# Stick-breaking attention scores: four f32 products per head against eight fp32r products

## What is computed

```python
def stick_breaking_attention(q, k, v):
    """A[t,s] = sigmoid(z_ts) * prod_{s<j<t} (1 - sigmoid(z_tj)), s < t."""
    z = jnp.einsum('bhqd,bhkd->bhqk', q_blk, kf) * scale
    mask = key_pos < qpos
    log1m = jnp.where(mask, jax.nn.log_sigmoid(-z), 0.0)
    excl = lax.cumsum(log1m, axis=3, reverse=True) - log1m
    a = jnp.where(mask, jnp.exp(jax.nn.log_sigmoid(z) + excl), 0.0)
    return jnp.einsum('bhqk,bhkd->bhqd', a, vf)
```

## Time and profile before

| | us |
|---|---|
| median of 3 runs | 2076.29 |
| lowest, highest | 2075.66, 2077.76 |
| the profiled execution's own time | 2076.51 |
| its span in the profile | 2074.7 |
| TensorE busy | 2026.1 |
| DVE busy | 919.0 |
| ACT busy | 909.0 |
| POOL busy | 848.9 |

### The profile page before, as it was taken

How to read it: one execution, slowest core, us unless ns; L and a number is a source line. 1 busy time by engine, 2 the same in 40 slices (tenths; PEclk the granted TensorE clock), 3 DMA queues, 4 the chain that set the end, 5 groups by cost and what they waited for, 6 DMA issues and landing times.

```text
span 2074.7 us, 23325 instructions
## 1 busy us (share of the span) xinstructions
PE 2026.1 (98%) x9356; PEld 1653.8 (80%) x9356; DVE 919.0 (44%) x1436; ACT 909.0 (44%) x1254; POOL 848.9 (41%) x672
## 2 busy tenths in 40 slices
PE   7999999989999998899999999999999999999999
PEld 6778778868888886788887888888877778888887
DVE  5633224244301315788785454155064544531551
ACT  6455444343223323664655443244266644432441
POOL 1243344436544543333333454444441244444442
PEclk9999999999999999999999999999999999999999
DMA  6122222323333332121212233333311222332332
GB/s 249 48 87 65 78 77 76 92 71 112 92 102 93 100 99 64 51 72 52 71 62 71 85 108 101 93 94 100 94 42 30 80 71 92 101 102 82 112 92 71
DMA packets 51659, 178.09 MB, mean 86 GB/s; under 512 B 5728, under 2 KB 8928, under 8 KB 51424
## 3 DMA queue, kind: packets, MB, share of 16 engines
q1 hardware_dynamic: 51552, 176.61, 27.3%
HBM read 174.49 MB, written 2.10 MB: 85 GB/s over the span
## 4 chain that ended last, share of the span: by engine, by line
PE 93%; DVE 3%; ACT 2%; POOL 1%; issue 1%; DMA 0%; SPq 0%; ACTq 0%
PE ps_gemm L225 24%; PE ps_gemm L227 23%; PE ps_gemm L226 23%; PE ps_attend L225 3%; PE ps_attend L227 3%; PE ps_attend L226 3%; PE ps_attend L1428 2%; PE ps_attend L756 1%; PE ps_attend L2208 1%; PE ps_attend L741 1%; PE ps_attend L2274 1%; PE ps_attend L2209 1%; PE ps_attend L258 1%; PE ps_gemm L1414 0%; PE ps_attend L1457 0%
## 5 line engine op out<-in xcount | busy, mean ns | idle before, releaser
L2467 POOL TENSOR_TENSOR weights_low<-weights_raw,weights_high 128x512 fp32r<-128x512 f32 (+1 forms) x334 | 423.1, 1267 | 1204.4 <-ACT weights_high L200 1203.9
L225 PE MATMUL ps_gemm<-normed_high,weights_high 128*128 128x512 f32 x1672 | 666.4, 399 | 14.2 <-DVE normed_low L287 12.0
L227 PE MATMUL ps_gemm<-normed_low,weights_high 128*128 128x512 f32 x1672 | 652.7, 390 | 0.0
L226 PE MATMUL ps_gemm<-normed_high,weights_low 128*128 128x512 f32 x1672 | 652.4, 390 | 0.0
L200 ACT ACTIVATE weights_high<-weights_raw 128x1024 fp32r<-128x1024 f32 (+1 forms) x341 | 340.8, 1006 | 462.1 <-PE ps_attend L227 220.0
L2468 POOL TENSOR_TENSOR weights_low<-weights_raw,weights_high 128x512 fp32r<-128x512 f32 (+1 forms) x334 | 441.3, 1321 | 0.0
L225 PEld LDWEIGHTS ps_gemm<-normed_high,weights_high 128*128 128x128 f32 x1672 | 315.3, 189 | 85.9 <-DVE normed_low L287 14.4
L226 PEld LDWEIGHTS ps_gemm<-normed_high,weights_low 128*128 128x128 f32 x1672 | 315.4, 189 | 66.4 <-issue 3.8
L227 PEld LDWEIGHTS ps_gemm<-normed_low,weights_high 128*128 128x128 f32 x1672 | 314.7, 188 | 66.3
L225 PE MATMUL ps_gemm<-operands_high_low,weights_high 128*128 128x512 f32 x552 | 217.5, 394 | 2.8 <-POOL weights_low L2468 2.4
L227 PE MATMUL ps_gemm<-operands_high_low,weights_high 128*128 128x512 f32 x552 | 215.7, 391 | 0.0
(11 more groups left out here) (283 smaller groups left out, 2086.0 us busy)
## 6 DMA issues: line engine op xcount, KB each, us to landing
weights_raw<-weights_full SPq DMA_DIRECT2D x317, 512.0 KB, 3.6
weights_raw<-weights_short SPq DMA_DIRECT2D x24, 128.0 KB, 2.0
residual<-x_tiles SPq DMA_DIRECT2D x4, 512.0 KB, 6.9
out_tiles<-residual SPq DMA_DIRECT2D x8, 256.0 KB, 2.1
parameters<-params SPq DMA_DIRECT2D x1, 1559.5 KB, 11.2
scratch<-memory_tiles SPq DMA_DIRECT2D x2, 512.0 KB, 5.7
scratch<-positions SPq DMA_DIRECT2D x1, 256.0 KB, 11.4
parameters<-params SPq DMA_DIRECT2D x1, 136.5 KB, 2.2
```

Of the source, the lines that this page charges most:

```text
L225: t.op.matmul(out, m.wh[:, c:c + P], xh, start=start and n == 0, stop=False, skip_group_check=True)
L226: t.op.matmul(out, m.wl[:, c:c + P], xh, start=False, stop=False, skip_group_check=True)
L227: ins = t.op.matmul(out, m.wh[:, c:c + P], xl, start=False, stop=stop and n == len(pairs) - 1, skip_group_check=True)
L2467: g.op.tensor_tensor(m.wl[:, a], m.raw[:, a], m.wh[:, a].bitcast(F32), ALU.subtract)
```

## The change

Each f32 product of the scores becomes two fp32r products. The first is stacked: 128 rows of contraction, in which the keys' tile holds the head's high keys in its own 64 partitions and its low keys in the other 64, and the queries' tile holds the high queries twice. It yields high times high plus low keys times high queries. The second has 64 rows: high keys times low queries. Low times low is left out.

For this ACT makes, per pair, four 64x512 copies of q (high queries of both heads, own rows and then the other rows) and two of k; DVE makes two low parts of q (into a new tile `ql`) and two low parts of k. Two stack tiles per head lie in unused tiles of `operands_high_low`. TensorE waits for both (`q_both` of ACT, `k_low` of DVE) before the scores of a head. On ACT one more weight unit is copied (`first + 4` in place of `first + 3`) before `act_stick_out`.

```diff
+        self.ql = sb("queries_low", TILE, F32R)
...
+def stick_stacks(m, hh):
+
+
+    return (m.high_tile(6), m.high_tile(7))[hh], (m.high_tile(19), m.high_tile(23))[hh]
+
+
+def own_and_other(hh):
+    return slice(64 * hh, 64 * hh + 64), slice(64 - 64 * hh, 128 - 64 * hh)
+
+
+def act_stick_queries(m, s, i):
+    q = stick_tiles(m)[0]
+    s.wait_ge(*m.V.at("stick", "q", i))
+    for own in (True, False):
+        for hh in range(2):
+            rows = own_and_other(hh)
+            ins = s.op.activation(stick_stacks(m, hh)[1][rows[0 if own else 1], :], q[rows[0], :], ACT.Copy)
+        ins.then_inc(*m.A.mark("stick", "q_high" if own else "q_both", i))
+
+
+def act_stick_keys(m, s, i):
+    k = stick_tiles(m)[1]
+    s.wait_ge(*m.V.at("stick", "k", i))
+    for hh in range(2):
+        own, _ = own_and_other(hh)
+        ins = s.op.activation(stick_stacks(m, hh)[0][own, :], k[own, :], ACT.Copy)
+    ins.then_inc(*m.A.mark("stick", "k_high", i))
+
+
+def dve_stick_parts(m, v, i, what):
+
+    src = stick_tiles(m)[0 if what == "q" else 1]
+    v.wait_ge(*m.A.at("stick", what + "_high", i))
+    for hh in range(2):
+        own, other = own_and_other(hh)
+        keys, queries = stick_stacks(m, hh)
+        out, high = (m.ql[own, :], queries[own, :]) if what == "q" else (keys[other, :], keys[own, :])
+        ins = v.op.tensor_tensor(out, src[own, :], high.bitcast(F32), ALU.subtract)
+    ins.then_inc(*m.V.mark("stick", what + "_low", i))
...
 def pe_stick_scores(m, t, i, hh):
...
-    t.wait_ge(*m.V.at("stick", "k", i))
+    t.wait_ge(*m.A.at("stick", "q_both", i))
+    t.wait_ge(*m.V.at("stick", "k_low", i))
     for kb in (0, 1, 3, 2):
-        w = S - kb * P
-        t.op.matmul(zb[:, ZOFF[kb]:ZOFF[kb] + w], k[r:r + 64, kb * P:(kb + 1) * P], q[r:r + 64, kb * P:S],
-                    start=kb != 3, stop=False, skip_group_check=True)
+        out, sl = zb[:, ZOFF[kb]:ZOFF[kb] + S - kb * P], slice(kb * P, (kb + 1) * P)
+        t.op.matmul(out, keys[:, sl], queries[:, kb * P:S], start=kb != 3, stop=False, skip_group_check=True)
+        t.op.matmul(out, keys[own, sl], m.ql[own, kb * P:S], start=False, stop=False, skip_group_check=True)
...
-    high_to(m, s, first + 3)
+    high_to(m, s, first + 4)
     if i:
         act_stick_out(m, s, i - 1)
+    act_stick_queries(m, s, i)
     high_to(m, s, first + 5)
+    act_stick_keys(m, s, i)
     act_stick_softplus(m, s, i, 0)
...
         if i and n == 0:
             dve_stick_low_out(m, v, i - 1)
+        if n < 2:
+            dve_stick_parts(m, v, i, name)
     softplus(0)
```

More of the change, by code:

```diff
@@ L728, in pe_stick_scores @@
 def pe_stick_scores(m, t, i, hh):
-    q, k, _, _, _ = stick_tiles(m)
+    keys, queries = stick_stacks(m, hh)
+    own, _ = own_and_other(hh)
     _, _, mask, ident = stick_matrices(m)
     zb = m.a_bank[:, 0:ZW]
-    r = 64 * hh
     if hh or i:
```

## The result

The changed kernel takes 2086.47 us (median of 5 runs, 2086.23 to 2091.93) against 2076.29 (5 runs too, with the same median as the three above); the ratio is 1.0053, 95% interval 1.0042 to 1.0065. It is slower, by more than was forecast. The median lies at the very end of the range, which was 2086.5; the ratio, which follows the means, gives 2087.3 and lies above it. The profiled execution is the slowest of the five: 2091.93, span 2090.1. It is 15.4 above the profiled execution of before.

A forecast was written before the change was run, and what follows sets the result against it. TensorE's instruction stream was taken as the bound, busy 98% of the span. 2076.5 + 1.4 (forms) + 3.8 (wait) + 1.7 (clock) + 0 = 2083.4, less 0.2 for the median: 2083.2 us, range 2070 to 2086.5.

The forecast's parts named there:

- The forms: TensorE's scores blocks: 0.20 us per change between 128-row and 64-row products, block 3.35 against 3.17, +1.4 us in all.
- Rival 2: Scores blocks: no drain between fp32r products of unlike form, so faster, -4.4 us, 2071.9; chance 0.15.
- The wait of pair 0: Before the first scores: TensorE waits for ACT's and DVE's new operand parts, low keys last, +3.8 us.
- Rival 3: Before the first scores: stall only 1.9 and no slow clock, +3.3 us, 2079.6; chance 0.14.
- Pairs 1 to 3: Before the later pairs' scores: low keys done 0.3 to 0.9 early, cost 0, upper bound 0.4 us each.
- Rivals 1: Behind pair 0's wait: the clock holds at 2.4 GHz, +5.2 us, 2081.5; chance 0.18.
- rival 4: Scores blocks: each fp32r product over 64 rows goes as two records, +5 more, 2088; chance 0.03.
- The clock: Behind pair 0's wait: a 3.4 us stretch at 1.2 GHz loses half, +1.7 us, bounds 0 and 1.7.
- upper bounds that meet: Whole kernel: several terms at their upper bounds together, a case left outside the forecast range ending at 2086.5.

The follow-up runs named there:

- masks_between: The kernel before, with each mask moved directly behind its own f32 product, same instructions in the same numbers: 2091.47 us, ratio 1.0081 to the kernel before.
- grouped: The changed kernel with the four stacked products of a block first, then the four of 64 rows: 2077.22 us, ratio 1.0001 to the kernel before.
- full rows: The changed kernel with the second product over 128 rows too, low queries in both halves of their tile: 2072.49 us, ratio 0.9982 to the kernel before.
- early: The changed kernel with pair 0's copies and low parts made during the cross attention, products still alternating: 2080.36 us, ratio 1.0019 to the kernel before.

## Why the prediction was right on the forms and the wait and wrong on the clock

- **The forms.** Right: 0.20 a change, a block of 3.35, +1.4 in all; the change was expected to pay at every product and does. Rival 2, no drain between fp32r products, is refuted by the timeline and by masks_between. The Trainium skill (TensorEngine Tiling (Array Packing), Key Properties) has the drain; the trace agrees, and adds the 0.20.
- **The wait of pair 0.** Right: 3.8 forecast, 3.8 measured, with low keys last. Rival 3, a stall of 1.9, is out. Pairs 1 to 3 wait for nothing: the low keys of pair 1 take 2.42 and end 0.5 before its scores. Rivals 1 and 4 are out as well: the clock did fall, and PE has 9356 records in both kernels, one for each new product. That rival 4's 2088 lies near the measured time is chance.
- **The clock.** This step failed. It read: a stretch of 3.4 us loses half, "+1.7 us, bounds 0 and 1.7". By medians the change costs 10.2 in all, which less 1.4 and 3.8 leaves 5.0 for the clock where 1.7 was forecast, and the upper bound was too small with it. Its size was taken from one place. Behind pair 0's wait the stretch was 10.2 long in both profiled executions of the change, 6.8 with f32 or grouped blocks behind the same wait, 3.4 with full rows. In these four kernels the clock came back sooner the fewer changes of form followed. That this is the cause is not shown: but for the change there is one execution of each, and at 45 us the same wait before the same products gave none, 3.4 and 6.8. What exactly the chip looks at, these runs don't tell. A stretch of this length stood in the trace of before as well, behind a wait of 2.1, though with a second wait of 5.0 in it, and the bounds of the term left it out:

```profile
436.00:446.00 10.00, 5.00 (x10) 2.79 (x10) 6.72 (x10) 6.16 (x9) 2.37 (x2) 0.51 0.18 54
```

- **A second error of the same step.** That a block can lower the clock with no wait was not considered. In the two profiled executions it came twice each, at up to 1.7 apiece, and in masks_between four times, where it costs about as much as the changes of form themselves. How the 5.0 of the median is divided between the stretch behind the wait and these falls is open, since both profiles of the change are of the longest of five executions; without the wait (early), 3.4 less 1.4 leaves 2.0 for the falls.
- **The range.** 2086.5 is not short of the upper bounds that meet, as the prediction says: it is their sum (2.1 + 5.2 + 1.7, and 3 x 0.4 for pairs 1 to 3, on 2076.3). With a bound of 5 to 8 for the clock it would have been 2090 to 2093.
- *The gain that the change was built on is there*: a block of eight products without a change of form takes 1.88 in place of 3.17. It is collected in full only when one form alone is used and the operands are ready.

## What to carry to other kernels

Count the changes of the array's form in a stream of products, not only their columns: at 0.20 us each, a product of 512 columns over half the rows between two over all rows took 0.42 here in place of 0.23, and one over all rows, with a copy in the other half, was cheaper. Group products of one form if they must be mixed. And where TensorE is the bound, a wait can cost more than its length, since the clock can fall behind it: the 3.8 of this case cost 5.5 with full rows, 6.2 grouped, 7.5 with the f32 products and 6 to 8 with the change. Take the range of such a term from all stretches at 1.2 GHz that the trace has, not from one. Look for slack ahead of the wait (here moments between ACT's kept copies) to prepare operands.

## What the runs showed of the hardware that I had not expected

The granted clock fell to 0.50 with no idle time of TensorE that the profile counts as a wait: four times in masks_between, once in early, twice in each profiled execution of the changed kernel. Each time it was in the last 1.0 us of a block with eight changes of form or within 0.6 behind it. It never came in the kernels with two changes or none between 120 and 340 us. By masks_between, which has the instructions of the kernel before in another order, it is the order that brings the falls.

The Trainium skill (TensorE: Matmul & The Clock Gate, A second HAM failure mode: psum-queue depth-cycling) reports of another kernel that small idle moments between groups of matmuls, if frequent, make the clock oscillate. The falls here are in line with it, with 0.20 lost at each change of form. That these losses act on the clock as idle moments is not shown: the profile has TensorE busy for the whole window (20.20 of 20.20 ahead of the fall at 144). Not settled is why one block is followed by a fall and the next, with the same instructions, is not.
